# The second layer's modulation, second and third thirds: from TensorE in the first mixer to VectorE in the dense rows

## What is computed

```python
def modulation(cvec, w_ada, b_ada):
    return jnp.split(jax.nn.silu(cvec) @ w_ada + b_ada, 6, axis=-1)
...
    for l in range(DEPTH):
        last = l == DEPTH - 1
        sh1, sc1, g1, sh2, sc2, g2 = [m[:, None, :] for m in modulation(c, w_ada[l], b_ada[l])]
        csh1, csc1, cg1, csh2, csc2, cg2 = modulation(c_ctx, w_ada[l], b_ada[l])
        h_lat = rmsnorm(x, norm1_g[l]) * (1.0 + sc1) + sh1
        h_ctx = rmsnorm(xc, norm1_g[l]) * (1.0 + csc1) + csh1
        o_lat, o_ctx = mixer(h_lat, h_ctx, ...)
        x = x + g1 * o_lat
        h_lat = rmsnorm(x, norm2_g[l]) * (1.0 + sc2) + sh2
```

## Time and profile before

| what | value |
|---|---|
| median of 3 runs | 1482.9 us (1482.24 to 1485.37) |
| profiled execution, its own time | 1484.85 us |
| its span, first to last instruction | 1483.0 us |
| TensorE busy | 1384.1 us, 93% of the span |
| VectorE busy | 525.7 us, 35% |
| ScalarE busy | 398.7 us, 27% |
| DMA | 395.92 MB, 267 GB/s on average |
| mean granted TensorE clock | 0.974 |

### The profile page before, as it was taken

One profiled execution on the slowest core, in us unless ns is written; L12 is line 12 of the kernel. 1 busy time (PEld: TensorE's weight loads), 2 busy tenths in 40 slices (PEclk: granted clock), 3 DMA queues, 4 the chain that ended last, 5 costly groups with the idle time before them and its releaser, 6 DMA issues.

```text
span 1483.0 us, 25756 instructions
## 1 busy us (share of the span) xinstructions
PE 1384.1 (93%) x11327; PEld 821.8 (55%) x11327; DVE 525.7 (35%) x954; ACT 398.7 (27%) x701; POOL 4.1 (0%) x8
## 2 busy tenths in 40 slices
PE   6899889999999999989898999999999998889886
PEld 3688657888888888878675343333333332223221
DVE  2799884523232333469864112011100010001022
ACT  3522485422222322376482111010110010000001
POOL 0000000000000000000000000000000000000010
PEclk9999899999999999999999999999999999999898
DMA  9997903532331052411418999999999999999995
GB/s 353 385 343 274 352 2 114 171 114 68 103 114 57 29 187 97 143 57 58 171 41 341 399 371 409 406 409 406 409 407 408 408 406 410 405 410 406 408 410 221
DMA packets 147031, 395.92 MB, mean 267 GB/s; under 512 B 7488, under 2 KB 38752, under 8 KB 146912
## 3 DMA queue, kind: packets, MB, share of 16 engines
q1 hardware_dynamic: 144000, 388.86, 68.7%
q10 hardware_dynamic: 2336, 3.24, 0.6%
q0 software_dynamic: 576, 2.10, 0.4%
HBM read 390.76 MB, written 3.41 MB: 266 GB/s over the span
## 4 chain that ended last, share of the span: by engine, by line
PE 77%; DMA 12%; DVE 6%; SPq 2%; ACT 2%; issue 1%; DVEq 0%; ACTq 0%
PE bank L1196 22%; DMA weight_ring<-in_exp_w 9%; PE bank L1154 8%; PE bank L1013 5%; PE bank L1014 5%; PE bank L1012 5%; PE bank L735 4%; PE bank L736 4%; PE bank L737 4%; DMA weight_ring<-in_w_ada 3%; PE bank L1021 3%; PE bank L1022 3%; PE bank L1023 3%; PE bank L1162 2%; PE bank L681 2%; DVE weight_ring L1865 2%
## 5 line engine op out<-in xcount | busy, mean ns | idle before, releaser
L1196 PE MATMUL bank<-weight_ring,gathered 128*32 128x512 f32 (+1 forms) x3840 | 402.2, 569 | 32.9 <-DMA weight_ring<-in_exp_w 27.1
L1196 PEld LDWEIGHTS bank<-weight_ring,gathered 128*32 128x32 f32 x3840 | 127.0, 112 | 283.0 <-issue 282.3
L2259 DVE TENSOR_TENSOR scratch<-scratch,bank 64x512 f32<-64x512 f32 (+1 forms) x60 | 38.4, 640 | 357.2 <-ACT scratch L1672 354.9
L1154 PE MATMUL bank<-weight_ring,scratch 128*32 128x512 f32 x1344 | 157.8, 593 | 2.2 <-DMA weight_ring<-in_exp_w 2.2
L1014 PE MATMUL bank<-slot_halves,slot_halves 128*128 128x512 f32 x336 | 130.9, 390 | 0.0
L1013 PE MATMUL bank<-hT_halves,slot_halves 128*128 128x512 f32 x336 | 130.9, 390 | 0.0
L1012 PE MATMUL bank<-slot_halves 128*128 128x512 f32 x320 | 124.8, 390 | 0.0
L1865 DVE SCALAR_TENSOR_TENSOR weight_ring<-scratch,conv_weights,weight_ring 128x512 f32<-128x512 f32 (+1 forms) x207 | 121.3, 637 | 2.6 <-ACT weight_ring L1453 0.7
L736 PE MATMUL bank<-hT_halves,slot_halves 128*128 128x512 f32 (+1 forms) x352 | 122.0, 347 | 0.0
L735 PE MATMUL bank<-slot_halves,slot_halves 128*128 128x512 f32 (+1 forms) x284 | 105.6, 372 | 8.1 <-DVE slot_halves L1772 5.2
L1154 PEld LDWEIGHTS bank<-weight_ring,scratch 128*32 128x32 f32 x1344 | 43.8, 110 | 100.3 <-issue 91.0
(11 more groups left out here) (303 smaller groups left out, 1576.1 us busy)
## 6 DMA issues: line engine op xcount, KB each, us to landing
weight_ring<-in_exp_w SPq DMA_DIRECT2D x216, 1024.0 KB, 18.5
weight_ring<-in_w_ada SPq DMA_DIRECT2D x24, 2048.0 KB, 13.5
weight_ring<-in_exp_w SPq DMA_DIRECT2D x64, 768.0 KB, 15.0
weight_ring<-in_ffn_w SPq DMA_DIRECT2D x33, 1024.0 KB, 5.4
weight_ring<-in_w_in SPq DMA_DIRECT2D x8, 1024.0 KB, 11.6
weight_ring<-in_w_out SPq DMA_DIRECT2D x4, 2048.0 KB, 11.2
weight_ring<-in_w_in SPq DMA_DIRECT2D x2, 3072.0 KB, 15.2
expert_rows<-scratch ACTq DMA_DIRECT2D x14, 128.0 KB, 6.0
```

The lines of the kernel that those rows point to most:

```text
L1154: i = mm(bank[6][quarter, :], at01[:, c0:c0 + BLOCK], w2[:, i_, half * 512:(half + 1) * 512], start=(first and i_ == 0), stop=(last and i_ ...
L1196: i = mm(ps[BLOCK * job:BLOCK * (job + 1), 0:cw], gathered_block(e, k, b), w[:, kk, a * cw:(a + 1) * cw], start=(k == 0), stop=(k == KT - 1))
```

## The change

The eight pieces (1, 1, n) and (1, 2, n) leave TensorE's list and the weight ring. Their weights now come as 16 transfers of 1 MB, two to a piece, into two buffers of their own, and VectorE multiplies them: for each of the 8 rows of channels one operation over 128 x 512 (`late_steps_done`), the first a TENSOR_SCALAR, the others SCALAR_TENSOR_TENSOR onto the same tile `late_acc`. Eight such steps are put into each of the dense rows 4 to 11, four before the row's product and four after the second `piece_rest`. Two rows after a piece's steps, TensorE sums its tile over the partitions with four matmuls of 2 columns (`late_sums`), in rows 6 to 13. Only the latent vector is multiplied. Some semaphores are shared between the layers to make room; that changes no order.

```diff
-MOE0 = 56
+MOE0 = 48
-MOD_TURNS = [(0, 0), (0, 1), (0, 2), (1, 1), (1, 2), (1, 0)]
+MOD_TURNS = [(0, 0), (0, 1), (0, 2), (1, 0)]
+LATE_PIECES = [(b, n) for b in (1, 2) for n in range(4)]
+LATE_ROW = 4
...
+def late_row_of(step):
+    return LATE_ROW + step // 8
...
+        late_in = [ring[:, OFF[3] + 4096:OFF[3] + 6144], ring[:, TAIL + 4096:TAIL + 6144]]
+        late_acc = [ring[:, OFF[2] + 4096 + i * 512:OFF[2] + 4608 + i * 512] for i in range(4)]
...
-        for n in range(8):
-            ada(1, 1 + n // 4, n % 4, [2, 3, 4][n % 3])
-            if n == 3:
-                out_projection(0, 0, 0)
+        out_projection(0, 0, 0)
...
+        def late_free_row(i):
+            return late_row_of(STEPS_OF_HALF[i - 2] - 1) + 0.9 if i >= 2 else 0
+        def fill_free_row(group):
+            return 2 * (group - STAGE) + 2 if group >= STAGE else -1
...
+            def late_weights(i):
+                piece, half = divmod(i, 2)
+                b, n = LATE_PIECES[piece]
+                if i == 0:
+                    sp.wait_ge(L[0]["wo_mm"], KT)
+                if i >= 2:
+                    sp.wait_ge(late_step, STEPS_OF_HALF[i - 2])
+                sp.dma_start(late_w[i % 2], k_major(t["w_ada"][1], 512 * (4 * b + n), 512 * (4 * b + n + 1))[
+                    :, 4 * half:4 * half + 4, :]).then_inc(late_landed[i % 2], 16)
...
+                while group is not None and waiting is not None and late_free_row(waiting) <= fill_free_row(group):
+                    late_weights(waiting)
+                    waiting = next(late, None)
...
+            def late_sums(piece):
+                b, n = LATE_PIECES[piece]
+                pe.wait_ge(late_step, STEPS_OF_PIECE[piece])
+                for j in range(4):
+                    for v in range(2 if b == 0 else 1):
+                        at = 4 * (4 * n + j) + 2 * v
+                        i = mm(bank[LATE_BANK[b]][:, at:at + 2], late_acc[late_place(piece, v)][:, j * P:(j + 1) * P],
+                               const("ones")[:, 0:2], start=True, stop=True)
+                i.then_inc(mod_mm, 1)
...
-                    if l == 0 and i_ == 5:
-                        modulate(1, 2, 3)
...
-                        modulate(1, 1, 0)
-                        modulate(1, 1, 1)
-                    if l == 0 and i_ == 2:
-                        modulate(1, 1, 2)
-                        modulate(1, 1, 3)
-                    if l == 0 and i_ == 3:
-                        turn_modulation(1, 1)
-                        modulate(1, 2, 0)
-                    if l == 0 and i_ == 4:
-                        modulate(1, 2, 1)
-                        modulate(1, 2, 2)
...
-                if l == 0:
-                    turn_modulation(1, 2)
...
+                        for done in range(len(LATE_PIECES)):
+                            if late_row_of(STEPS_OF_PIECE[done] - 1) + 2 == n:
+                                late_sums(done)
...
-                    if l == 0 and st == 2:
-                        modulation_rows(1, 1)
-                    if l == 0 and st == 5:
-                        modulation_rows(1, 2)
...
+            def late_steps_done(begin, end):
+                for s in range(begin, min(end, len(LATE_STEPS))):
+                    piece, half, k, v = LATE_STEPS[s]
+                    i = 2 * piece + half
+                    if s == 0 or LATE_STEPS[s - 1][0:2] != (piece, half):
+                        dve.wait_ge(late_landed[i % 2], 16 * (i // 2 + 1))
+                    dst = late_acc[late_place(piece, v)]
+                    w, x = late_w[i % 2][:, k % 4, :], silu_c[:, 2 * k + v:2 * k + v + 1]
+                    if k == 0:
+                        held_by_piece = [q for q in range(piece) if late_place(q, 0) // 2 == late_place(piece, 0) // 2 or
+                                         LATE_PIECES[q][0] and late_place(q, 0) == late_place(piece, v)]
+                        if held_by_piece:
+                            dve.wait_ge(mod_mm, len(MOD_PIECES) + held_by_piece[-1] + 1)
+                        ts(dst, w, x, None, ALU.mult).then_inc(late_step, 1)
+                    else:
+                        dve.wait_ge(late_step, LATE_STEPS.index((piece, (k - 1) // 4, k - 1, v)) + 1)
+                        stt(out=dst, in0=w, scalar=x, in1=dst, op0=ALU.mult, op1=ALU.add).then_inc(late_step, 1)
...
-                    if l == 0 and st == 3:
-                        modulation(1, 1)
...
-                if l == 0:
-                    modulation(1, 2)
...
                         if 0 < n < NF - 1:
                             piece_rest(2 * n + 2)
+                            if s >= 0:
+                                late_steps_done(s, s + 4)
...
                             piece_rest(2 * n + 3)
+                            if s >= 0:
+                                late_steps_done(s + 4, s + 8)
```

More of the change, by code:

```diff
@@ L76, with late_steps @@
 SELECTS = len(GATHERS) + 1
+def late_steps():
+    steps = []
+    for piece, (b, n) in enumerate(LATE_PIECES):
+        for half in range(2):
+            for v in range(2 if b == 0 else 1):
+                for k in range(4):
+                    steps.append((piece, half, 4 * half + k, v))
+    order = []
+    for piece in range(len(LATE_PIECES)):
+        for half in range(2):
+            mine = [s for s in steps if s[0] == piece and s[1] == half]
+            order += sorted(mine, key=lambda s: (s[2], s[3]))
+    return order
+LATE_STEPS = late_steps()
+STEPS_OF_PIECE = [sum(s[0] <= piece for s in LATE_STEPS) for piece in range(len(LATE_PIECES))]
+STEPS_OF_HALF = [sum((s[0], s[1]) <= (i // 2, i % 2) for s in LATE_STEPS) for i in range(2 * len(LATE_PIECES))]
+def late_row_of(step):
+    return LATE_ROW + step // 8
 def unit_at(v):
@@ L311, in backbone @@
         eps_ready = sem("eps_ready")
+        late_landed = [sem(f"late_weights_{i}") for i in range(2)]
+        late_step = sem("late_step")
         def k_major(w, a, b):
@@ L516, in fill_sums, with late_place @@
             return sums(g - 1, 2 - spot % 2)
+        DONE_BEFORE = 4
+        LATE_BANK = [5, 6, 7] if (0, 0) in LATE_PIECES else [None, 4, 7]
+        def late_place(piece, v):
+            return 2 * (piece % 2) + v if LATE_PIECES[piece][0] == 0 else piece % 4
         FIRST_FILL_BANK = [7, 6, 5, 3]
@@ L557, in _ @@
             sp.dma_start(xtok[:, 2:4, :], t["ctx"][0].rearrange("(n p) d -> p n d", p=P)).then_inc(ctx_in, 16)
+            def late_weights(i):
[7 more added lines that the diff above has]
+                    :, 4 * half:4 * half + 4, :]).then_inc(late_landed[i % 2], 16)
+            late = iter(range(2 * len(LATE_PIECES)))
+            waiting = next(late)
             for n, (parts, free) in enumerate(fills):
+                group = (F[0]["w13"] + F[0]["w2"]).index(n) if n in F[0]["w13"] + F[0]["w2"] else None
+                while group is not None and waiting is not None and late_free_row(waiting) <= fill_free_row(group):
+                    late_weights(waiting)
+                    waiting = next(late, None)
                 if n >= SLOTS:
@@ L2040, in _ @@
                             piece_rest(2 * n + 3)
+                            if s >= 0:
+                                late_steps_done(s + 4, s + 8)
+                        for b in range(3):
+                            if (b, 3) in LATE_PIECES and late_row_of(STEPS_OF_PIECE[LATE_PIECES.index((b, 3))] - 1) + 2 == n:
+                                late_modulation(b)
                     for n in range(2, NF):
```

44 lines of the change are left out of this document (27 added, 17 removed).

## The result

| | before | after |
|---|---|---|
| median | 1482.87 us (1481.93 to 1485.37) | 1490.26 us (1487.67 to 1492.43) |
| ratio | | 1.0044, 95% interval 1.0033 to 1.0055 |
| profiled execution, own time and span | 1484.85, 1483.0 us | 1490.34, 1488.4 us |

The change makes the kernel slower by 6.5 us (4.9 to 8.2). The forecast was 1486.9 us with a range of 1483.3 to 1490.6.

The account below looks back on a forecast made before the run. TensorE was taken to bound the dense part and VectorE's list the first mixer. Sums +7.2 us less the mixer's gain of 3.15 us made +4.05 us, forecast 1486.9 us, range 1483.3 to 1490.6 us.

Parts of the forecast that it names:

- the forecast case: Whole kernel: the sum as worked out, +4.05 us, 1485.9 to 1489.2 us; chance 0.50.
- VectorE late after a hold: Dense rows 6, 8, 10, 12: TensorE waits for the low half, +2 to +4 us more, 1489 to 1491; chance 0.14.
- a mixer that gives nothing: First mixer: low clock falls on more than tile 12, no gain, +7, 1490 us; chance 0.09.
- The gain of the mixer: First mixer and attention: removing the eight calls gains 3.15 us in all, bounds 2.1 and 5.7.
- The 3.65 us: First mixer, before 166.40: VectorE's wait for `rotate(3)` behind the call at 162.16 goes, 3.65 us.
- The clock's share: First mixer, tile 12: half clock after TensorE's 7.2 us wait takes back 2.1 us, bounds 1.6 and 2.7.
- a clock that stays up: First mixer: clock does not fall in the 7.2 us wait; +1.95, 1484.8 us; chance 0.13.
- The sums: Dense rows 6 to 13: four fp32 matmuls per row cost 0.9 us, eight times, 7.2 us.
- The cheap bound from the transposes: Dense rows: sums priced like four transposes, 0.44 us plus 0.1, 4.3 us in all; as a rival, chance 0.09.
- Steps, transfers and holds: Dense rows: VectorE's steps, the 1 MB transfers and waits for earlier sums add no cost.
- The margin after a hold: Dense rows: low half after a held step done 0.45 us before TensorE wants it, four times over.
- TensorE's pace: First mixer: TensorE, not VectorE, sets the pace, so all 17 us go; -10, 1473 us; chance 0.05.

Follow-up runs that it names:

- mixer_alone: Changed kernel with only the eight calls' removal from the first mixer kept, no late transfers, steps or sums; ratio 0.9984 to the kernel before.
- after_again: The changed kernel run once more, unaltered; ratio 1.0039 to the kernel before.
- kept_warm_wide: Changed kernel plus 29 unused full-width 128 x 512 matmuls in TensorE's wait before the first rotation; ratio 1.0022 to the kernel before.
- kept_warm: Changed kernel plus 96 small unused matmuls in TensorE's wait before the first rotation; ratio 1.0034 to the kernel before.
- steps_no_sums: Changed kernel with late transfers and all 64 VectorE steps, but without TensorE's sums and the holds; ratio 0.9989 to the kernel before.
- no_hold: Changed kernel with a piece's first step waiting only for the piece that used the very same tile; ratio 1.0039 to the kernel before.
- scores_first: Kernel before, with call (1, 2, 3), its transposes, bias and gains moved behind the first scores; ratio 0.9979 to the kernel before.
- sums_twice: Changed kernel with each group of four sums done twice over; ratio 1.0094 to the kernel before.
- last_third: Changed kernel with only pieces (1, 2, n) on VectorE, calls (1, 1, n) staying in the first mixer; ratio 0.9992 to the kernel before.
- sums_at_turn: Only the last third on VectorE, its four groups of sums moved from the dense rows to the turn of the layers; ratio 0.9978 to the kernel before.

## Why the prediction held, and what it missed

- **Direction and size.** Slower was forecast with a chance of 0.64. The sum came to +4.05 us; the marks give +5.33 and the ratio 6.5. The mechanism is the forecast's, but the median of 1490.26 us lies above the 1485.9 to 1489.2 that the forecast case was given, and inside the range by 0.3 us only because the range was drawn to take in slower rivals (VectorE late after a hold, a mixer that gives nothing), which did not happen. That part is luck. Of the distance, 1.2 us are the stall below. Another 1.2 us, between the marks and the ratio, are not explained; the executions of one kernel spread over 3.4 us (before) and 4.8 us (after), so they may be nothing but scatter.
- **The gain of the mixer**, 3.15 us forecast, was 3.40 (mixer_alone 3.43, after_again 3.10). The waits are those forecast: 7.25 us of idle TensorE (7.2 said), a wait for the root of 2.74 us (2.4). The first maximum comes 2.64 us earlier (2.75) and attention is 0.76 us shorter (0.4, bounds 0 and 0.9), but this division does not repeat: in after_again it is 3.25 us earlier and 0.15 us longer.
- **The 3.65 us** of waiting for the fourth rotation went, as said. The prediction knew that 1.1 us of them were a late transfer. It did not see that, by the estimate above, another 1.6 us were a clock at 0.50: it used the 3.10 us of this very call as the price of the low clock, and did not ask what made the clock low there.
- **The clock's share**, taken at 2.1 us, measured 2.4 (kept_warm_wide; 2.1 to 2.7 with the scatter). The row from 40.00 to 43.20 in the earlier trace rows was the right one to go by. The rule of the Trainium skill, "TensorE: Matmul & The Clock Gate", section "HAM oscillation — how this bites in real kernels", by which a long wait inside work is paid for at half clock, agrees with the trace of after. It is not the whole story here: the clock also fell behind waits of 1.10 us (before, at 162.16) and 1.87 us (kept_warm). The rivals of a clock that stays up, and of a mixer that gives nothing, are both out.
- **The sums**, 7.2 us forecast, were 7.49. L830's 0.79 us in the earlier trace rows was the right neighbour: the chain of after holds each group for 0.79 us too. The cheap bound from the transposes was not.
- **Steps, transfers and holds** cost nothing, as said (steps_no_sums, no_hold). The margin after a hold, put at 0.45 us, was 0.74. A transfer was put at 5.4 us and took 6.5, more than the 6.3 us that the prediction gave the tightest step; even so VectorE waits for no transfer from 280 to 640 us.
- **What the sum left out.** It lists only what the change moves. The stall of 0.80 us in TensorE's list, 1.22 us by the stretch, has no term in it, and is most of the 1.3 us between 4.05 and 5.33. It repeats at the same record in after_again and stands 64 records later in kept_warm (timeline of TensorE there):

```profile
273.85 3.25 PE L743 MATMUL bank<-weight_ring,silu_c 128*32 128x128 f32 x109
278.02 0.85 PE L743 MATMUL bank<-weight_ring,silu_c 128*32 128x128 f32 x19 [0.92 <-issue]
```

All three go with a late transfer of instructions. Count from the first call (1, 0, 0). DMA queue 8, which moves instructions, brings a packet of 16 KB at 47.5 to 50.0 us in before, kept_warm_wide, scores_first and no_hold, and the stretch takes 55.04 to 55.07 us. It brings it at 50.2 to 50.5 in steps_no_sums, mixer_alone, sums_twice, last_third and the two runs with sums at the turn, and the stretch takes 55.18 to 55.50. In after_again it comes at 50.9 (55.99), in after at 51.2 (56.26), in kept_warm at 53.2 (56.38). The stall of these three ends 1.3 to 1.4 us after the packet has landed. By their number these packets are TensorE's: there are 88 in after, for 10871 matmul records and as many weight loads, 247 to a packet. In kept_warm 384 more stand ahead of this place, about a packet and a half, and its stall stands 64 matmul records, about half a packet, further on. So TensorE very likely waits there for its own instructions, but this is argued from thirteen traces and not shown: no run moved that packet on purpose, and why it comes late, while the weight queue keeps the DMA engines full, is open.

- **"TensorE's pace"** as a rival is out by mixer_alone: 17 us of calls gone give 3.43 us. scores_first says the same: moving one call, removing none, brings the first maximum forward by 4.5 us, more than taking away all eight.

## What to carry to other kernels

Work taken off an engine that waits for another is worth only the other's waits: here 17 us of matmuls gave 3.4. What is put back where TensorE never waits costs its full price, however small: eight groups of four 2-column matmuls, 7.5 us. So look first for an order in which the waiting engine is served sooner (scores_first removes nothing and is faster), and for places where the receiver is idle (sums_at_turn), and price them at the clock of that place.

Emptying an engine can cost its clock. Half of the change, which left TensorE busy at the critical wait, gained 5.1 us in the mixer where all of it gained 3.4.

## What was not expected of the hardware

- The clock fell to 0.50 although TensorE had hardly been idle: in before behind a wait of 1.10 us (162.16), in kept_warm behind 5.45 us of small matmuls and 1.87 us of waiting, and in sums_at_turn at the start of 4.90 us of 2-column matmuls, behind waits of 0.28 and 0.56 us; it then stayed low from 642 to 648 us, with TensorE busy for 2.00 of every 2.00 us. With 6.87 us of 512-column matmuls and 0.45 us of waiting it stayed at 1.00 (kept_warm_wide).
- Adding matmuls whose product nobody uses made the changed kernel 2.4 us faster in the mixer (kept_warm_wide against after).
- TensorE stood still for 0.53 to 0.92 us, waiting for nothing that the profile shows, in the three traces in which a 16 KB packet of instructions came latest, and in none of the ten others in these calls.
